# Moving cleared products on TensorE to the front of a hybrid decoder step

## What is computed

```python
def _trunk_layer(x, c, ...):
    sh1, sc1, gt1, sh2, sc2, gt2 = split(silu(c) @ w_mod + b_mod, 6)
    h = rmsnorm(x, g_pre_mix) * (1 + sc1) + sh1
    ... = split(h @ w_in, IN_SPLITS)          # HGRN2, differential attention, gates
    o_a, o_b = hgrn2(...), diff_attention(...)
    merged = sigmoid(gate_a) * (o_a @ w_proj_a) + sigmoid(gate_b) * (o_b @ w_proj_b)
    x = x + gt1 * rmsnorm(merged @ w_out, g_post_mix)
    h2 = rmsnorm(x, g_pre_ffn) * (1 + sc2) + sh2
    return x + gt2 * rmsnorm(moe_top4_of_32(h2), g_post_ffn)
```

## Time and profile before

| | us |
|---|---|
| median of three runs | 1261.01 |
| lowest and highest run | 1259.24, 1261.58 |
| span of the profiled execution | 1258.5 |
| PE busy in the span | 1102.0 (88%) |
| DVE busy | 588.2 (47%) |
| ACT busy | 230.7 (18%) |

### The profile page before, as it was taken

The page is one execution under the profiler, slowest core; times in us unless marked ns, Lnnn a source line. Parts: engine busy times, 40 slices in busy tenths (PEclk is TensorE's granted clock), DMA queues, the critical chain, the costliest instruction groups (busy, mean ns, idle before and its releaser), DMA issues.

```text
span 1258.5 us, 23992 instructions
## 1 busy us (share of the span) xinstructions
PE 1102.0 (88%) x9856; PEld 456.6 (36%) x9856; DVE 588.2 (47%) x1166; ACT 230.7 (18%) x420; POOL 68.5 (5%) x126
## 2 busy tenths in 40 slices
PE   8999999999988697996887979999966995667996
PEld 4776777785322131321222322333211331112332
DVE  3536744444654252563353544666532552332654
ACT  3002510141311110220111211112100211100212
POOL 0312020250100000000000000000000000000000
PEclk9999999999989897998798999999988998888999
DMA  9979994599899999999999999999999999999995
GB/s 342 312 245 347 317 339 154 187 384 366 284 428 429 426 429 426 429 425 429 426 428 428 428 426 393 409 424 427 428 427 428 427 426 430 424 431 425 428 428 236
DMA packets 67619, 485.30 MB, mean 386 GB/s; under 512 B 6421, under 2 KB 29450, under 8 KB 40762
## 3 DMA queue, kind: packets, MB, share of 16 engines
q1 hardware_dynamic: 59312, 461.07, 88.9%
q0 software_dynamic: 7104, 19.65, 4.9%
q10 hardware_dynamic: 1130, 3.51, 0.8%
HBM read 479.47 MB, written 4.72 MB: 385 GB/s over the span
## 4 chain that ended last, share of the span: by engine, by line
DMA 45%; PE 27%; DVE 1%; issue 0%; DVEq 0%; ACT 0%; ACTq 0%
DMA big<-in_w_down 26%; PE PB L1247 13%; DMA big<-in_w_gate_up 13%; PE PB L1274 7%; DMA hTG<-in_w_down 5%; PE PB L1214 2%; PE PB L1201 2%; PE PB L1206 1%; PE PB L1229 1%; PE PB L1221 1%; PE PB L1240 0%; PE PB L1186 0%; PE PB L1232 0%; DVE big L1623 0%; DVE big L1620 0%
## 5 line engine op out<-in xcount | busy, mean ns | idle before, releaser
L1247 PE MATMUL PB<-big,cst 128*32 128x512 f32 x2768 | 355.0, 657 | 109.2 <-DMA big<-in_w_gate_up 109.2
L2189 DVE TENSOR_TENSOR tok<-PB,cst 32x512 f32<-32x512 f32 x188 | 129.1, 687 | 261.7 <-ACT cst L1554 259.8
L1247 PEld LDWEIGHTS PB<-big,cst 128*32 128x32 f32 x2768 | 89.0, 115 | 345.2 <-issue 181.1
L1274 PE MATMUL PB<-big,cst 128*32 128x512 f32 x1408 | 166.6, 602 | 12.8 <-DMA big<-in_w_down 12.7
L2165 DVE TENSOR_SCALAR mod<-PB 64x256 f32<-64x256 f32 x96 | 41.0, 427 | 209.1 <-PE PB L1247 208.4
L756 PE MATMUL PB<-hTG,big 128*128 128x264 f32 x576 | 136.5, 391 | 0.4 <-DVE hTG L1617 0.4
L756 PEld LDWEIGHTS PB<-hTG,big 128*128 128x128 f32 x576 | 106.9, 190 | 27.3 <-issue 10.8
L1544 ACT ACTIVATE mod<-PB 64x256 f32<-64x256 f32 x96 | 36.1, 376 | 422.3 <-PE PB L1247 421.7
L1274 PEld LDWEIGHTS PB<-big,cst 128*32 128x32 f32 x1408 | 39.2, 110 | 96.8 <-issue 65.8
L1201 PE MATMUL PB<-wide,att 128*32 128x256 f32 x784 | 57.9, 415 | 5.1 <-DVE att L2159 4.9
L1554 ACT ACTIVATE cst<-PB 128x512 f32<-128x512 f32 x48 | 28.7, 597 | 178.2 <-PE PB L1274 178.2
(11 more groups left out here) (378 smaller groups left out, 970.9 us busy)
## 6 DMA issues: line engine op xcount, KB each, us to landing
big<-in_w_gate_up SPq DMA_DIRECT2D x115, 2048.0 KB, 31.0
big<-in_w_down SPq DMA_DIRECT2D x57, 2048.0 KB, 23.9
hTG<-in_w_gate_up SPq DMA_DIRECT2D x13, 2048.0 KB, 37.1
big<-in_w_mod SPq DMA_DIRECT2D x24, 1024.0 KB, 7.5
big<-in_w_in SPq DMA_DIRECT2D x22, 1024.0 KB, 9.2
hTG<-in_w_down SPq DMA_DIRECT2D x6, 2048.0 KB, 24.0
wide<-in_cache_k POOLq DMA_DIRECT2D x16, 256.0 KB, 6.8
big<-in_w_out SPq DMA_DIRECT2D x4, 1024.0 KB, 10.5
```

The costliest lines, as they stand in the source:

```text
L1247: mm = pe.matmul(GU[32 * j:32 * j + 32, :], mo["xT"][:, (2 * u + r) * M:(2 * u + r + 1) * M], groups(w[:, r * 2 * D:(r + 1) * 2 * D])[:, j ...
L1274: mm = pe.matmul(DN[32 * j:32 * j + 32, :], mo["actT"][:, (4 * u + r) * M:(4 * u + r + 1) * M], w[:, r * D + half * 512:r * D + (half + 1) ...
L2189: mm = dve.tensor_tensor(mo["y"][rows, :], DN[rows, :], mo["y_part"][other, :], ALU.add)
```

## The change

TensorE's first run of cleared products grows from 6 to 17, ahead of the transpose "vt". The run behind that transpose grows from 4 to 5, and the run behind the bias product shrinks from 7 to 2. Together they are 24 where they were 17.

```diff
             pe.wait_ge(S("zeros_ready"), 1)
-            idle_products(6)
+            idle_products(17)
             pe.wait_ge(S("small_loaded"), 16 * 8)
             full(tr(begin("vt")[:, 0:NV], vrows[0:NV, :], NV))
...
-            idle_products(4)
+            idle_products(5)
             scale_bias()
-            idle_products(7)
+            idle_products(2)
             scale_part(0)
             scale_part(1)
```

## The result

The changed kernel took 1265.65 us (median of 10 runs, 1259.57 to 1272.15) beside 1260.17 us for the kernel before (10 runs, 1259.15 to 1265.75). The ratio is 1.0037, with a 95% interval of 1.0020 to 1.0053: 5.5 us slower, where 1.0 us faster was forecast with a range up to 1263.0.

The account below looks back on a forecast made before the run. TensorE was taken to set the pace until 335 us, the DMA weight stream from 400. Transposes 0.5 us earlier plus 0.54 in the first four made 1.0: 1261.0 - 1.0 = 1260.0 us, range 1257.8 to 1263.0.

Parts of the forecast that it names:

- The run of 17: TensorE's opening: cleared products start at 1.49 us, the clock rises at 6.54, and they end at 7.7.
- The late "vt": Opening: "vt" starts 3.3 us later, at 7.7, so the norm's `xn` comes at 15.0 and its 2.2 us slack is gone.
- The sum of the forecast case: Opening: transposes begin 0.5 us earlier and the first four win 0.54, together 1.0 us; chance 0.47.
- The clock rises and falls again: Rival, chance 0.24: the clock falls in pauses around part 0, part 1 takes 1.94 us; 1261.0 to 1261.7 us.
- The 0.84 for no change: Whole kernel: the chance given to a measurement telling no difference, beside 0.09 for faster and 0.07 for slower.
- The passing on: Behind the opening: a microsecond won by 24 us moves the mixer, the weight stream's start and the end with it.
- Cleared products that don't lift the clock: Rival, chance 0.19: the run ends at 8.8, part 0 starts at 13.05; 0.9 to 1.4 us slower.
- Won and lost again: Rival, chance 0.10: the 1.0 us won ends in a longer TensorE wait for DVE; 1261.0 us.
- The wait at L903: TensorE's 1.1 us wait for DVE, where the gain could be lost if DVE's side doesn't move with it.

Follow-up runs that it names:

- twelve dense products: Changed kernel without its cleared products behind "vt" and the bias product, with twelve between scale part 1 and the first transposes; 1264.63 us, ratio 1.0021.
- (6, 16, 2): Changed kernel with six cleared products ahead of "vt" instead of 17, sixteen behind it instead of five, two behind the bias product; 1260.27 us, ratio 0.9992.
- eight products: Changed kernel with eight cleared products added between scale part 1 and the first transposes; 1263.89 us, ratio 1.0028.

## Why the prediction was wrong

**The run of 17: right.** It lifts the clock in every profile of a kernel with it; "vt" started at 6.99 to 8.39 us in these nine profiles, for 7.7 predicted.

**The late "vt": right in size.** Where the clock held, the transposes waited for `xn` and started at 15.25, for 15.0 predicted. In the slow profile they didn't wait for it.

**The sum of the forecast case: right at the projection, and of little use.** With the clock held, the projection came 0.79 us earlier (23.98 for 24.77), against 1.0. But by their times 15 of 22 runs weren't that case.

**"The clock rises and falls again": right mechanism, wrong price, too small a chance.** This is the step that failed. I gave it 0.24 and 0 to 0.7 us. Its place was right: part 1 at 1.93 behind pauses of 1.09 and 1.49 us, which I had put at 0.9 and 1.5. I thought the fall unlikely because the pauses were nearer to the 1.35 us of the earlier trace rows than to the 2.96: I judged each pause by its length. The runs don't bear that out, with 2.98 us held, 2.26 not, and in the mixer a fall right behind one of 1.00. And I let the clock rise again 5.05 us after part 1 began, the figure of the earlier trace rows, where TensorE ran products without transposes among them, the first sixteen in the form of a scale part. Here it ran transposes and parts, and the clock stayed low for 17 us, from 12.28 to 29.35, ten of them fully busy: 3.9 us at the projection instead of 0.7. The Trainium skill, in "TensorE: Matmul & The Clock Gate" on the PE-mode transpose, says that transposes don't count as busy in the way that matmuls do; the low stretch agrees, and the narrow times with twelve dense products fit it. In the earlier trace rows the clock rose among the transposes, behind a part, and the next four ran at the upper level (2.16 us), so the rule isn't the whole of it; no run here had the opening without its transposes.

**That the fall comes from the pauses** rests on counts more than on one profile. The five kernels in which the clock was raised ahead of part 0 and a pause of the changed kernel is filled or gone have 5 of 60 runs over 1263.5 us; the changed kernel has 15 of 22, and the run of 17 with nothing behind it 9 of 12.

**One profile taken for the kernel: the error beneath.** The earlier trace rows show the faster opening of before. The slower one, which before has in 37 of 109 runs, stood in no row, and three timed runs of 1259.24 to 1261.58 us hid it. So I had no row for a clock that stays low through all the transposes, and compared one outcome of before with several of the changed kernel. The 0.84 for no change rested on that.

**The passing on: right for the loss, not borne out for the gain.** What the opening lost, the span lost. But in the profile of the changed kernel whose clock held, 0.79 us won at the projection were 0.52 us when PE resumed after its longest pause (349.21 for 349.73), and the span was 1259.0 us, 0.5 us longer than that of before. The six faster of its twelve runs have a median of 1260.34 us, the 24 faster runs of before beside them 1259.78. So the forecast 1.0 us isn't seen in the time even where the forecast case came:

```profile
349.21 1.93 PE L1201 MATMUL PB<-wide,att 128*32 128x256 f32 x16 [4.90 <-DVE att L2159]
```

**Cleared products that don't lift the clock: excluded** by the 1.07 of part 0. **Won and lost again: open.** The wait at L903 isn't the place (1.2 us in the profile whose clock held, for 1.1), but in that profile the gain did get lost behind the opening.

Open: whether the share of slower runs really differs between sets of runs (1, 13, 11 and 12 in 10, 35, 35 and 29 of before), of which the last three ran on different chips; what eight products miss that twelve have, beyond their number; what sets the moment at which a pause brings the clock down; and why (6, 16, 2), whose transposes began at 14.30 instead of 15.51, has a median of 1260.27 us, above the middle (1259.5) of the 22 faster runs of before beside it.

## What to carry to other kernels

Work put in to raise TensorE's clock is spent faster once the clock is up, so it has to last, at the upper pace, until the real work comes without pauses; dummy products belong into the pauses that are left, not ahead of them. Before predicting microseconds in an opening, look at more than one execution: a median over two groups moves by the share of the groups, and a profile shows one member of one of them. Price a low clock by rows of the same kind of work, and by more than one of them, since a busy share alone doesn't tell whether that work will bring it back: the same opening of the kernel before did in one profile and didn't in another.

## What the runs showed of the hardware

Products of cleared operands can lift the clock: in the changed kernel's profile it rose about 3.9 us after the first of them (near 5.4 against 1.50, an estimate from the pace: seventeen products in 5.78 us). In three pieces, with "vt" and the bias product between them, seventeen hadn't lifted it by 10.66 us. An engine that the profile shows as fully busy, from 14 to 24 us, was left at 1.2 GHz (a granted clock of 0.50) all that time. And the clock held over a pause of 2.98 us in one profile and fell right behind one of 1.00 us in another.
